# A third fold of seven half-size products, and the MLPs' last sums added at another place

## The chip, the cores and the metric

The kernel runs on one core of a Trainium2 chip. The metric is the device time of one execution in microseconds (us), as the median of several. The engines are named as in the profile: PE is TensorE (matrix products), DVE is VectorE, ACT is ScalarE, POOL is GpSimd, and SP is the engine that issues most DMAs. A bank is one of the eight banks of PSUM, into which PE writes; each holds 128 x 512 float32 numbers.

## The reference

A sequence of 512 tokens with 1024 channels goes through three layers. Their matrices, in the order of the program:

```python
h = layer_norm(a*x + dsa_mixer(x))                 # layer 1, indexed sparse attention
h = layer_norm(a*h + square(relu(h @ w_up)) @ w_down)      # MLP "m1", 4096 hidden
h = layer_norm(a*h + gla_mixer(h))                 # layer 2, gated linear attention
h = layer_norm(a*h + square(relu(h @ w_up)) @ w_down)      # MLP "m2", 4096 hidden
x = x + g1 * (concat(attention(.), mlstm(.)) @ w_out)      # second block
x = x + g2 * ((silu(h @ w_gate) * (h @ w_up)) @ w_down)    # FFN "m3", 2816 hidden
out = rms_norm(x)
```

Everything is float32. The vectors g1, g2 and the shifts and scales of the second block come from one product with w_ada, which the kernel spreads over the MLPs ("ada").

## The kernel before

**Precision.** A float32 product is made of three on PE: each matrix is split into a high half (rounded, written by ACT) and a low half (what is left, written by DVE), and high x high, high x low and low x high are added in a bank. So a weight chunk of 1 MB goes through a fixed row of steps: SP fetches it into one of three `raw` buffers (L3378), ACT writes its high half `wh` (L1482), DVE its low half `wl` (L2212), and PE may read it. A raw buffer is free when its last reader is done, and only then does SP issue the next fetch, in the order of the chunks.

**The MLPs m1 and m2.** The 32 hidden tiles of 128 are worked on in eight units of four. In a cycle PE makes the hidden tiles of unit n (`gemm_T`, L746 to L748) and then the down product of unit n-1. ACT squares the hidden tiles (L1620, L1623). The result is gathered in `h` by DVE (L2428). Some units also carry a chunk of w_ada, which DVE multiplies into `A` (L2198).

**The fold.** For units 1 to 6 the down product, a product of 2x2 blocks, is made by `fold` (L968 to L970) with seven block products P1 to P7 in place of eight (Winograd's scheme): 7 x 12 = 84 matmuls in place of 96. It needs sums of blocks. Those of the hidden tiles are made by POOL (`hidden_sums`), those of the weights by DVE in place in the raw buffers (`weight_sums`, L2413, L2416, L2418, L2421). So a fold has four weight chunks: the left one, the right one with its first sum, the left with its sums, and the last sum; the last two are made of the raw buffers of the first two. P1, P6 and P7 are gathered in one bank after the other ("chain"): P7 may start when DVE has added P6, P6 when it has added P1. P4 and P5 are "lasting": their four banks gather all six units, and DVE adds each of them to two corners of the result at the end of unit 7, six adds L2428 after the last weights.

**The ends of m1 and m2.** Unit 7's down product is made corner by corner: (0,0), (0,1), then (1,0) and so on, a corner being a row block of 128 tokens and half of the channels (`cross` in m1, L770 to L772). While PE is at the next corners, DVE adds the corner to `h` (L2388), takes its statistics (L2270) and, after both halves of a row block, works out the scale of the norm (L2274 to L2288, "scale"). Ahead of the corners stands the ada sum (L906).

**The FFN m3.** Its 22 hidden tiles come in six units, FG = 2, 4, 4, 4, 4, 4 tiles. ACT makes silu(gate), DVE the product with the other branch (L3205) and the low half (L3208). The down product is plain: 22 tiles x 4 x 2 x 3 = 528 matmuls; DVE gathers it (L3188), and in the second-last unit multiplies by g2 and adds to the residual (L3193, L3195). The last unit goes by corners and each is finished at once (L3175, L3178). Two weight slots take turns.

The order of every engine's queue is written out by hand; a helper `take` prepares a fixed number of chunks ahead, and `weights(i)` all up to i.

## Time and profile before

| | |
|---|---|
| median of 3 runs | 1837.14 us (1834.05 to 1839.25) |
| profiled execution | 1838.28 us |
| its span in the trace | 1836.1 us |
| granted TensorE clock, mean | 0.995 |
| PE busy | 1797.3 us, 98% of the span |
| DVE busy | 1248.5 us, 68% |
| ACT busy | 840.4 us, 46% |
| POOL busy | 228.5 us, 12% |

The span lies within the execution, 2.2 us of which are outside it. ACT squares its first hidden tile of m1 at 261 us of the span and of m2 at 871; the last fold of m1 ends at 557 us, that of m2 at 1155; DVE makes the first product of m3 at 1491.

### The profile page before, as it was taken

How to read it: one execution, taken by the hardware profiler on the slowest of the kernel's cores; microseconds unless marked ns; L12 is line 12 of the kernel's file. 1: busy time of each engine (PE TensorE's matmuls, PEld its weight loads, DVE VectorE, ACT ScalarE, POOL GpSimd, SP SyncE). 2: the span in 40 equal slices, each digit the busy share in tenths (PEclk: the TensorE clock that was granted, in tenths of full speed). 3: DMA queues.
4: the chain of work that ended last, by engine and by line, in shares of the span. 5: the costliest groups of instructions: out<-in, count | busy, mean ns of one | idle time of the engine just before them, and what ended most of it. 6: DMA issues, size and time to landing. Idle time of an engine off the chain costs nothing.

```text
span 1836.1 us, 22790 instructions
## 1 busy us (share of the span) xinstructions
PE 1797.3 (98%) x8996; PEld 1465.0 (80%) x8996; DVE 1248.5 (68%) x2048; ACT 840.4 (46%) x1313; POOL 228.5 (12%) x172
## 2 busy tenths in 40 slices
PE   9999999999999999999999999899999999999998
PEld 7775788878887888878888888778757898888886
DVE  4997666888888677476777777886667644433438
ACT  4548453445443443555344444465566442222223
POOL 0241002111110054000222221000012000000001
PEclk9999999999999999999999999999999999999999
DMA  6221405544443121140533433133102313233221
GB/s 215 70 70 36 150 24 184 181 163 138 168 153 117 47 74 65 46 161 24 207 115 115 136 122 133 49 105 102 47 24 70 126 47 115 94 107 98 92 92 46
DMA packets 120330, 189.34 MB, mean 103 GB/s; under 512 B 7816, under 2 KB 72552, under 8 KB 117152
## 3 DMA queue, kind: packets, MB, share of 16 engines
q1 hardware_dynamic: 118688, 182.81, 30.0%
q0 software_dynamic: 1392, 4.82, 0.8%
q8 instruction: 71, 1.16, 0.3%
q14 instruction: 35, 0.29, 0.1%
q10 hardware_dynamic: 144, 0.26, 0.0%
HBM read 185.72 MB, written 2.16 MB: 102 GB/s over the span
## 4 chain that ended last, share of the span: by engine, by line
PE 71%; DVE 16%; DMA 6%; ACT 5%; issue 3%; DVEq 0%; SPq 0%; ACTq 0%
PE bank L746 8%; PE bank L748 8%; PE bank L747 8%; DMA raw<-in_mlp_w_up 4%; DVE wl L2212 3%; PE bank L720 3%; PE bank L722 3%; PE bank L721 3%; PE bank L970 2%; ACT wh L1482 2%; PE bank L968 2%; PE bank L969 2%; DMA raw<-in_mlp_w_down 2%; PE bank L1058 2%; DVE A L2198 2%
## 5 line engine op out<-in xcount | busy, mean ns | idle before, releaser
L2212 DVE TENSOR_TENSOR wl<-raw,wh 128x2048 fp32r<-128x2048 f32 (+2 forms) x161 | 355.2, 2209 | 214.4 <-ACT wh L1482 214.2
L1482 ACT ACTIVATE wh<-raw 128x2048 fp32r<-128x2048 f32 (+1 forms) x166 | 302.0, 1826 | 323.0 <-DMA raw<-in_mlp_w_up 107.4
L746 PE MATMUL bank<-xh,wh 128*128 128x512 f32 (+1 forms) x872 | 341.2, 391 | 0.0
L748 PE MATMUL bank<-xl,wh 128*128 128x512 f32 (+1 forms) x872 | 340.3, 390 | 0.0
L747 PE MATMUL bank<-xh,wl 128*128 128x512 f32 (+1 forms) x872 | 340.3, 390 | 0.0
L746 PEld LDWEIGHTS bank<-xh,wh 128*128 128x128 f32 (+1 forms) x872 | 164.0, 188 | 37.2 <-DVE h L2428 1.7
L748 PEld LDWEIGHTS bank<-xl,wh 128*128 128x128 f32 (+1 forms) x872 | 163.9, 188 | 34.9
L747 PEld LDWEIGHTS bank<-xh,wl 128*128 128x128 f32 (+1 forms) x872 | 164.0, 188 | 34.3
L720 PE MATMUL bank<-wh,xh 128*128 128x512 f32 (+1 forms) x352 | 138.0, 392 | 0.5 <-DVE wl L2212 0.5
L722 PE MATMUL bank<-wh,xl 128*128 128x512 f32 (+1 forms) x352 | 134.1, 381 | 0.0
L721 PE MATMUL bank<-wl,xh 128*128 128x512 f32 (+1 forms) x352 | 133.9, 380 | 0.0
L968 PE MATMUL bank<-wh,uh 128*128 128x512 f32 x336 | 130.8, 389 | 0.1
L969 PE MATMUL bank<-wl,uh 128*128 128x512 f32 x336 | 130.7, 389 | 0.0
L970 PE MATMUL bank<-wh,ul 128*128 128x512 f32 x336 | 130.7, 389 | 0.0
L2428 DVE TENSOR_TENSOR h<-h,bank 128x512 f32<-128x512 f32 x132 | 86.0, 681 | 43.8 <-PE bank L970 43.7
L1584 ACT ACTIVATE A<-bank 128x512 f32<-128x512 f32 (+4 forms) x106 | 51.4, 490 | 74.9 <-PE bank L722 31.8
L1620 ACT ACTIVATE A<-bank 128x512 f32<-128x512 f32 x64 | 38.0, 593 | 90.3 <-PE bank L748 73.8
L720 PEld LDWEIGHTS bank<-wh,xh 128*128 128x128 f32 x352 | 66.2, 188 | 15.1 <-issue 2.6
L722 PEld LDWEIGHTS bank<-wh,xl 128*128 128x128 f32 x352 | 66.1, 188 | 12.8
L721 PEld LDWEIGHTS bank<-wl,xh 128*128 128x128 f32 x352 | 66.2, 188 | 11.5
L848 PE MATMUL bank<-xh,wh 128*128 128x256 f32 x256 | 73.6, 287 | 1.0 <-DVE xl L2263 0.6
L968 PEld LDWEIGHTS bank<-wh,uh 128*128 128x128 f32 x336 | 63.1, 188 | 13.6 <-issue 0.6
(401 smaller groups left out, 3512.3 us busy)
## 6 DMA issues: line engine op xcount, KB each, us to landing
raw<-in_mlp_w_up SPq DMA_DIRECT2D x32, 1024.0 KB, 5.6
raw<-in_mlp_w_down SPq DMA_DIRECT2D x32, 1024.0 KB, 5.2
raw<-in_w_ada SPq DMA_DIRECT2D x24, 1024.0 KB, 5.0
raw<-in_b_w_in SPq DMA_DIRECT2D x12, 1024.0 KB, 5.2
raw<-in_w_gate SPq DMA_DIRECT2D x11, 1024.0 KB, 5.3
raw<-in_w_up SPq DMA_DIRECT2D x11, 1024.0 KB, 5.3
raw<-in_w_in SPq DMA_DIRECT2D x10, 1024.0 KB, 5.0
raw<-in_w_down SPq DMA_DIRECT2D x10, 1024.0 KB, 5.0
```

The lines of the kernel that those rows point to most:

```text
L720: pe.matmul(o, X, H[:, k, :], start=kk == 0, stop=False)
L721: pe.matmul(o, X, L[:, k, :], start=False, stop=False)
L722: step = pe.matmul(o, Y, H[:, k, :], start=False, stop=kk == 7)
L746: pe.matmul(o, H[:, k, c], xh[:, k, :], start=k == 0, stop=False)
L747: pe.matmul(o, L[:, k, c], xh[:, k, :], start=False, stop=False)
L748: step = pe.matmul(o, H[:, k, c], xl[:, k, :], start=False, stop=k == 7)
L968: pe.matmul(o, X, H[:, k0 + k, :], start=not begun and k == 0, stop=False, skip_group_check=on)
L969: pe.matmul(o, X, L[:, k0 + k, :], start=False, stop=False, skip_group_check=on)
L970: step = pe.matmul(o, Y, H[:, k0 + k, :], start=False, stop=ends and k == 1, skip_group_check=on)
L1482: act.activation(slots[slot_of[i]][0][:, 0:n], raw_of(i)[:, 0:n], ACT.Copy).then_inc(*s_high.up(i))
L2212: dve.tensor_tensor(L[:, 0:n], raw_of(i)[:, 0:n], H[:, 0:n].bitcast(F), ALU.subtract).then_inc(*s_low.up(i))
L2428: dve.tensor_tensor(hv, hv, ps, ALU.add).then_inc(*s_row.up(name, ((key, "down", 6), t, c)))
```

## The change

Four things change.

1. m3 has five units, of 4, 4, 4, 4 and 6 tiles. The down product of the first four is made by `fold`, under the key m3, with weight sums, hidden sums on POOL and lasting banks like those of m1; the last unit's six tiles are made directly, corner by corner, 18 matmuls each. There are three weight slots in turn and a sixth slot for the fold's half-size chunk.
2. A fold's chunks stand in another order in all three: left, left with sums, right with its sum, last sum (before: left, right, left with sums, last sum). In m1 and m2 the products come as P1, P2, P6, P5, P7, P4, P3. The left raw buffer is released by the last weight sum, too.
3. In m1 and m2 the lasting sums of P4 and P5 for the row blocks 2 and 3 leave the unit 7: in m1 they are added after the scale of row block 0, in m2 after the norm of row block 0.
4. The four lasting banks go back to the pool of banks only at the end of the last fold.

```diff
-FG = [(0, 2), (2, 4), (6, 4), (10, 4), (14, 4), (18, 4)]
+FG = [(0, 4), (4, 4), (8, 4), (12, 4), (16, 6)]
...
+    def plan_fold(key, d, m, r0):
+
+        folds[key, d] = len(chunks)
+        for c in range(2):
+            plan(m, r0, 4, c * 512, 512)
+            slot_of[len(chunks)] = turn[0]
+            turn.append(turn.pop(0))
+            chunks.append(([], (4, 2)[c], 512))
...
+        def released(i):
+
+            kd, part = fold_of.get(i, (0, None))
+            if part == 0:
+                return [low_of(i + 1), s_step.at(("fold", kd, 3))]
+            return [low_of(i + 1 if part else i)]
...
-        ORDER = (P1, P2, P6, P4, P7, P5, P3)
+        ORDER = {"m1": (P1, P2, P6, P5, P7, P4, P3), "m2": (P1, P2, P6, P5, P7, P4, P3),
+                 "m3": (P1, P2, P6, P4, P7, P5, P3)}
...
-                weights(first + 1)
-                    w.wait_ge(*low_of(first + 1))
-                    dve.tensor_tensor(R0, R1, L0, ALU.subtract).then_inc(*s_step.up(("fold", (key, d), 3)))
-                    weights(first + 2)
...
+            def last_weight_sum(key, d):
+
+                first = folds[key, d]
+                L0, L1, R0, R1 = halves(first)
+                weights(first + 2)
+                w.wait_ge(*low_of(first + 2))
+                dve.tensor_tensor(R0, R1, L0, ALU.subtract).then_inc(*s_step.up(("fold", (key, d), 3)))
...
-                        lasting(P4, 2, 0, True)
-                        lasting(P5, 2, 1, True)
                     owed()
+
+                def last_sums():
+                    lasting(P4, 2, 0, True)
+                    lasting(P5, 2, 1, True)
+
+                return last_sums
...
                     scale(t)
+                    if amid and t == 0:
+                        amid()
                     ada_sum()
...
+            product(0, 0)
+            product(0, 1)
+            cur.take(low)
+            product(0, 2)
+            product(0, 3)
+            cur.take(low)
...
+            cur.take(low, 0)
+            product(LASTF, 4)
+            product(LASTF, 5)
+            gated(3, 0)
+            cur.take(low, 0)
+            last_low(4)
+            last_low(5)
+            gated(3, 1)
+            cur.take(low, 0)
```

`product` is what L3205 does before, `gated` is L3193 and L3195 of before, `last_low` is L3208.

What this does to the queues, at three places. First DVE in a fold of m1, unit 2. wl2 and wl without a number are weight slots; raw<-raw rows are the weight sums. Before, the second L2212 is the right chunk and the third the left with its sums:

```order
L2212 TENSOR_TENSOR wl<-raw,wh 128x2048
L2413 TENSOR_TENSOR raw<-raw 128x1024
L2416 TENSOR_TENSOR raw<-raw 128x1024
L2418 TENSOR_TENSOR raw<-raw 128x1024
L2212 TENSOR_TENSOR wl<-raw,wh 128x2048
L2421 TENSOR_TENSOR raw<-raw 128x1024
L2212 TENSOR_TENSOR wl2<-raw,wh2 128x2048
L2428 TENSOR_TENSOR h<-h,bank6 128x512
```

The same place in the changed kernel (low halves now L2235, sums L2422 to L2435, adds L2448):

```order
L2235 TENSOR_TENSOR wl<-raw,wh 128x2048
L2422 TENSOR_TENSOR raw<-raw 128x1024
L2425 TENSOR_TENSOR raw<-raw 128x1024
L2427 TENSOR_TENSOR raw<-raw 128x1024
L2235 TENSOR_TENSOR wl2<-raw,wh2 128x2048
L2235 TENSOR_TENSOR wl<-raw,wh 128x2048
L2435 TENSOR_TENSOR raw<-raw 128x1024
L2448 TENSOR_TENSOR h<-h,bank6 128x512
```

The low half of the left sums (wl2) has moved from the third place to the first after the three sums; the right chunk and the last sum stand behind it.

Second, DVE at the end of m1, before. The six adds h<-h,bank are P3's (banks 6 and 1) and the four lasting ones (7, 2, 0, 4); wl3 is the last weight chunk of unit 7, the next three are those of the layer after it, L2388 is the first corner:

```order
L2212 TENSOR_TENSOR wl3<-raw,wh3 128x2048
L2428 TENSOR_TENSOR h<-h,bank6 128x512
L2428 TENSOR_TENSOR h<-h,bank1 128x512
L2428 TENSOR_TENSOR h<-h,bank7 128x512
L2428 TENSOR_TENSOR h<-h,bank2 128x512
L2428 TENSOR_TENSOR h<-h,bank0 128x512
L2428 TENSOR_TENSOR h<-h,bank4 128x512
L2212 TENSOR_TENSOR wl<-raw,wh 128x2048 x2
L2212 TENSOR_TENSOR wal<-raw,wal 128x128
L2388 TENSOR_TENSOR h<-h,bank2 128x512
```

In the changed kernel, from the same chunk on:

```order
L2235 TENSOR_TENSOR wl3<-raw,wh3 128x2048
L2442 TENSOR_TENSOR ul<-A,uh 128x512
L2475 TENSOR_TENSOR h<-h 128x512 x2
L2448 TENSOR_TENSOR h<-h,bank6 128x512
L2448 TENSOR_TENSOR h<-h,bank1 128x512
L2235 TENSOR_TENSOR wl<-raw,wh 128x2048 x2
L2235 TENSOR_TENSOR wal<-raw,wal 128x128
L2398 TENSOR_TENSOR h<-h,bank3 128x512
```

and, fifteen small instructions later, at the end of row block 0's scale:

```order
L2338 SCALAR_TENSOR_TENSOR rsa<-rsy,rsh 128x1
L2345 SCALAR_TENSOR_TENSOR small<-rsa,rsy 128x1
L2296 SCALAR_TENSOR_TENSOR small<-mv,small 128x1
L2448 TENSOR_TENSOR h<-h,bank0 128x512
L2448 TENSOR_TENSOR h<-h,bank4 128x512
L2448 TENSOR_TENSOR h<-h,bank7 128x512
L2448 TENSOR_TENSOR h<-h,bank2 128x512
```

Banks 0, 4, 7 and 2 are the lasting ones; their adds stand behind two weight chunks, two corners and a scale. PE's corner (1,0) takes bank 0.

Third, DVE at the start of m3, before (L3205 is a product of hidden tiles, L3208 its low half):

```order
L2212 TENSOR_TENSOR wl<-raw,wh 128x2048
L3205 TENSOR_TENSOR A<-A,bank5 128x512
L3208 TENSOR_TENSOR ul<-A,uh 128x512
L3205 TENSOR_TENSOR A<-A,bank7 128x512
L3208 TENSOR_TENSOR ul<-A,uh 128x512
L2212 TENSOR_TENSOR wl<-raw,wh 128x2048
L2212 TENSOR_TENSOR wl<-raw,wh 128x2048
L3205 TENSOR_TENSOR A<-A,bank0 128x512
```

and in the changed kernel, where the third L2235 is the gate chunk of unit 1:

```order
L2235 TENSOR_TENSOR wl2<-raw,wh2 128x2048
L3198 TENSOR_TENSOR A<-A,bank7 128x512
L3198 TENSOR_TENSOR A<-A,bank6 128x512
L2235 TENSOR_TENSOR wl<-raw,wh 128x2048
L3198 TENSOR_TENSOR A<-A,bank2 128x512
L3198 TENSOR_TENSOR A<-A,bank5 128x512
L2235 TENSOR_TENSOR wl<-raw,wh 128x2048
```

A chunk that PE reads next stands ahead of the products of hidden tiles before, and behind them now. In the last unit of the changed kernel the same holds for a down chunk (L3198 are the products of tiles 4 and 5, L3235 and L3237 a `gated`):

```order
L2235 TENSOR_TENSOR wl<-raw,wh 128x2048
L3198 TENSOR_TENSOR A<-A,bank2 128x512
L3198 TENSOR_TENSOR A<-A,bank5 128x512
L3235 TENSOR_TENSOR A<-A 128x512
L3237 TENSOR_TENSOR h<-h,A 128x512
L2235 TENSOR_TENSOR wl2<-raw,wh2 128x2048
L3242 TENSOR_TENSOR ul<-A,uh 128x512 x2
```

The first L2235 is the chunk of tiles 0 and 1, the second that of tiles 2 to 5 for the left half of the channels.

## Rows read from the trace of the kernel before

**Rows 1.** The page's line of PE and the others: busy time and share of the span by engine.

```profile
PE 1797.3 (98%) x8996; PEld 1465.0 (80%) x8996; DVE 1248.5 (68%) x2048; ACT 840.4 (46%) x1313; POOL 228.5 (12%) x172
```

**Rows 2.** Waits of PE, longest first: us in total, times, longest.

```profile
PE bank L906 <- DVE h L2428: 3.7, 1, 3.7
PE bank L770 <- DVE h L2428: 3.5, 1, 3.5
```

**Rows 3.** Timeline of PE: start us, us, instruction; a fold's start and end, another's P6.

```profile
331.86 0.39 PE L968 MATMUL bank<-wh,uh 128*128 128x512 f32 x1
...
350.89 0.39 PE L746 MATMUL bank<-xh,wh 128*128 128x512 f32 x1
...
378.33 0.47 PE L968 MATMUL bank<-wh,uh 128*128 128x512 f32 x1
```

**Rows 4.** Timeline of DVE in m1's folds, last one m2's; in brackets idle time before, and releaser.

```profile
377.51 1.28 DVE L2428 TENSOR_TENSOR h<-h,bank 128x512 f32<-128x512 f32 x2
...
449.03 1.23 DVE L2413 TENSOR_TENSOR raw<-raw 128x1024 f32<-128x1024 f32 x1 [0.37 <-DMA raw<-in_mlp_w_down]
...
451.62 1.23 DVE L2418 TENSOR_TENSOR raw<-raw 128x1024 f32<-128x1024 f32 x1
452.77 2.28 DVE L2212 TENSOR_TENSOR wl<-raw,wh 128x2048 fp32r<-128x2048 f32 x1
455.09 1.23 DVE L2421 TENSOR_TENSOR raw<-raw 128x1024 f32<-128x1024 f32 x1
456.23 2.28 DVE L2212 TENSOR_TENSOR wl<-raw,wh 128x2048 fp32r<-128x2048 f32 x1
...
466.23 2.73 DVE L2212 TENSOR_TENSOR wl<-raw,wh 128x2048 fp32r<-128x2048 f32 x1 [0.82 <-ACT wh L1482]
468.87 3.38 DVE L2198 SCALAR_TENSOR_TENSOR A<-raw,small,A 128x2048 f32<-128x2048 f32 x1
...
489.94 1.23 DVE L2413 TENSOR_TENSOR raw<-raw 128x1024 f32<-128x1024 f32 x1 [0.51 <-DMA raw<-in_mlp_w_down]
...
1013.83 0.69 DVE L2428 TENSOR_TENSOR h<-h,bank 128x512 f32<-128x512 f32 x1 [3.39 <-PE bank L970]
```

**Rows 5.** Timeline of SP and of ACT in the same fold: fetches and high halves.

```profile
458.54 0.37 SPq L3378 DMA_DIRECT2D raw<-in_mlp_w_up  x1
...
452.88 1.92 ACT L1482 ACTIVATE wh<-raw 128x2048 fp32r<-128x2048 f32 x1 [0.67 <-DVE raw L2418]
...
464.20 1.92 ACT L1482 ACTIVATE wh<-raw 128x2048 fp32r<-128x2048 f32 x1 [1.59 <-DMA raw<-in_mlp_w_up]
```

**Rows 6.** Timelines of ACT, DVE and PE at the end of m1.

```profile
560.28 1.91 ACT L1482 ACTIVATE wh<-raw 128x2048 fp32r<-128x2048 f32 x1 [1.01 <-DMA raw<-in_b_w_in]
...
568.96 0.69 DVE L2388 TENSOR_TENSOR h<-h,bank 128x512 f32<-128x512 f32 x1 [0.47 <-PE bank L772]
...
572.45 0.16 DVE L2288 SCALAR_TENSOR_TENSOR small<-mv,small 128x1 f32<-128x1 f32 x1
...
569.12 0.47 PE L770 MATMUL bank<-wh,uh 128*128 128x512 f32 x1
```

**Rows 7.** End of m2: DVE and PE timelines; windows (us, busy and count by engine, PEclk).

```profile
1157.20 3.67 DVE L2428 TENSOR_TENSOR h<-h,bank 128x512 f32<-128x512 f32 x6
...
1159.13 0.80 PE L770 MATMUL bank<-wh,uh 128*128 128x512 f32 x1 [3.54 <-DVE h L2428]
...
1164.42 0.46 PE L770 MATMUL bank<-wh,uh 128*128 128x512 f32 x1
...
1169.00:1202.00 33.00, 30.84 (x144) 24.27 (x144) 30.23 (x73) 16.68 (x35) 0.00 (x0) 1.00 0.10 32
...
1159.00:1163.00 4.00, 3.87 (x9) 3.11 (x10) 4.00 (x6) 1.88 (x3) 0.00 (x0) 0.50 0.48 133
```

**Rows 8.** m3: a window of it, and one instruction of DVE's timeline.

```profile
1490.00:1829.00 339.00, 338.84 (x1501) 280.47 (x1500) 149.35 (x164) 91.21 (x95) 9.05 (x7) 1.00 0.28 90
...
1507.92 0.69 DVE L3205 TENSOR_TENSOR A<-A,bank 128x512 f32<-128x512 f32 x1 [0.64 <-PE bank L748]
```

More of the change, by code:

```diff
@@ new lines, in silu @@
+            def silu(n, i):
+                q, j = i // 2, i % 2
+                w.wait_ge(*s_gemm.at((("gate", n, q), j)))
+                if i > 3:
+                    w.wait_ge(*s_xlow.at(("m3", "u", i - 4)))
+                elif n:
+                    w.wait_ge(*s_xlow.at(("m3", "U", n - 1, P3 if q else P5)))
+                act.activation(rb[:, i % 4, :], bank[banks.of[("gate", n, q), j]][:, :], ACT.Silu).then_inc(*s_act.up(("gate", n, i)))
+                banks.read[("gate", n, q), j] = s_act.at(("gate", n, i))
@@ new lines, in scalar_program @@
+            cur.take(high)
+            high_of("m3", 0, P1)
+            high_of("m3", 0, P4)
+            high_of("m3", 0, P2)
+            for n in range(1, LASTF):
+                first = folds["m3", n - 1]
+                cur.take(high, 0)
+                cur.take(high, 0)
+                for s in (P6, P7, P5, P3):
+                    high_of("m3", n - 1, s)
+                cur.take(high, 0)
+                silu(n, 0)
+                silu(n, 1)
+                cur.take(high, 0)
+                weights(first)
+                silu(n, 2)
+                silu(n, 3)
+                weights(first + 2)
+                high_of("m3", n, P4)
+                high_of("m3", n, P1)
+                weights(first + 3)
+                high_of("m3", n, P2)
+                cur.used = first + 4
+                weights(first + 5)
@@ new lines, in scalar_program @@
+            first = folds["m3", LASTF - 1]
+            cur.take(high, 0)
+            cur.take(high, 0)
+            for s in (P6, P7, P5, P3):
+                high_of("m3", LASTF - 1, s)
+            weights(first)
+            silu(LASTF, 0)
+            silu(LASTF, 1)
+            weights(first + 3)
+            cur.used = first + 4
+            cur.take(high, 0)
+            cur.take(high, 0)
+            last_high(0)
+            last_high(1)
+            cur.take(high, 0)
+            silu(LASTF, 2)
@@ new lines, in vector_program, with added @@
+            last = {}
+            def added(d, s):
+                t0, c = TO[s]
+                for t in (t0, t0 + 1):
+                    name, where = ("m3", "Q", d, s, t - t0), sum_of("m3", d, s, t - t0)
+                    ps = bank[banks.of[where]][:, :]
+                    w.wait_ge(*s_gemm.at(("m3", "P", d, s, t - t0)))
+                    if (t, c) in last:
+                        w.wait_ge(*s_row.at(last[t, c]))
+                        dve.tensor_tensor(fv(t, c), fv(t, c), ps, ALU.add).then_inc(*s_row.up(name))
+                    else:
+                        dve.tensor_copy(fv(t, c), ps).then_inc(*s_row.up(name))
+                    last[t, c] = name
+                    if s in (P2, P7, P3):
+                        banks.read[where] = s_row.at(name)
@@ new lines, in lasting @@
+            def lasting(s, t0, c, base):
+                for t in (t0, t0 + 1):
+                    name, where = ("m3", "E", s, t, c), sum_of("m3", LASTF - 1, s, t - t0)
+                    w.wait_ge(*s_gemm.at(("m3", "P", LASTF - 1, s, t - t0)))
+                    w.wait_ge(*s_row.at(last[t, base]))
+                    dve.tensor_tensor(fv(t, c), fv(t, base), bank[banks.of[where]][:, :], ALU.add).then_inc(*s_row.up(name))
+                    last[t, c] = name
+                    if t0:
+                        banks.read[where] = s_row.at(name)
@@ new lines, in vector_program @@
+            d, first = LASTF - 1, folds["m3", LASTF - 1]
+            cur.take(low, 0)
+            cur.take(low, 0)
+            for s in (P6, P7, P5, P3):
+                low_half_of("m3", d, s)
+            weight_sums("m3", d)
+            weights(first + 1)
+            product(LASTF, 0)
+            product(LASTF, 1)
+            added(d, P1)
+            last_weight_sum("m3", d)
+            added(d, P2)
+            added(d, P6)
+            weights(first + 3)
+            added(d, P7)
@@ new lines, in vector_program @@
+            weights(first + 4)
+            lasting(P5, 0, 1, 1)
+            lasting(P5, 2, 1, 0)
+            lasting(P4, 2, 0, 0)
+            cur.used = first + 4
+            cur.take(low, 0)
+            cur.take(low, 0)
+            last_low(0)
+            last_low(1)
+            added(d, P3)
+            gated(0, 0)
+            gated(1, 0)
+            cur.take(low, 0)
+            gated(0, 1)
+            product(LASTF, 2)
+            product(LASTF, 3)
+            gated(1, 1)
+            cur.take(low, 0)
@@ L3357, in gpsimd_program @@
             pool.dma_start(fg, final_norm_g_2.partition_broadcast(P)).then_inc(s_gb, 16)
+            for d in range(LASTF):
+                hidden_sums("m3", d)
             w.wait_ge(s_gb, 16 * G_FIN)
@@ L3411, in sync_program @@
             for before, i in zip(fetched, fetched[NRAW:]):
-                w.wait_ge(*low_of(before + 2 if before in fold_of else before))
+                for read in released(before):
+                    w.wait_ge(*read)
                 fetch(i)
```

466 lines of the change are left out of this document (217 added, 249 removed).

## The prediction

> **What bounds the kernel now.** I read the page's busy shares first: PE is busy 98% of the span [rows 1]. PE is the bound, and a change pays if it takes matmuls away or fills PE's gaps; DVE and ACT matter where they make PE wait. The matmul's price comes from starts, since their shown durations overlap: a fold of 84 starts at 331.86 and what follows it at 350.89, so 19.03/84 = 0.2266 us each [rows 3]. Next, PE's waits, longest first. The two longest are 3.7 and 3.5 us, for adds of DVE at the ends of m1 and m2 [rows 2]; six such adds stand there in one row of 3.67 us [rows 7].
>
> Then I looked for what nearly bounds PE, since such a thing turns into a wait when it is moved. It is in m1's folds. Follow one weight buffer through the timelines [rows 4, 5]: the first sum L2413 starts at 449.03, three sums run to 452.85, the right chunk's low half, the last sum and the left sums' low half follow with no gap to 458.51; SP fetches the next chunk into the buffer just freed at 458.54; it has landed and ACT starts on it at 464.20, idle before that for the DMA; DVE's low half starts at 466.23, idle before that for ACT; an L2198 of 3.38 us ends at 472.25 and frees the next buffer; two more fetches later the next first sum starts at 489.94, again idle before that for its DMA. No step of this ring waits for PE, and its round takes 40.91 us. PE's own cycle there is 96 matmuls of hidden tiles and 84 of the fold, 180 x 0.2266 = 40.8 us. The two are equal: the ring has no slack. In one fold it already shows: DVE's two adds of P1 start at 377.51, and PE's P6, which waits for the first, starts at 378.33, 0.24 us later than the pitch puts it [rows 3, 4].
>
> **The change, part by part.** All differences are against the profiled execution, 1838.28 us (span 1836.1); the median of the runs is 1837.14, 1.1 lower.
>
> *Fewer matmuls in m3.* Sixteen tiles in four folds: 4 x 84 = 336; six tiles direct: 6 x 24 = 144; 480 in place of 528. 48 x 0.2266 = -10.9 us, all on the path: in m3 PE is busy 338.84 of 339 us [rows 8]. The sums, hidden sums and adds that pay for it lie on DVE, ACT and POOL; DVE is busy there only 149 of 339 us, so I cost them at nothing, but for the two places below. The corners at the end are longer than DVE's work on them; I take -0.4 for the 0.5 us by which DVE is late there.
>
> *The start of m3.* The low half of unit 1's gate chunk is now queued behind the products of tiles 2 and 3 (third place of the order above). The last product waits for PE's last matmul before that chunk, and PE needs the chunk at once: signal 0.1 + product 0.69 [rows 8] + low half 2.28 [rows 4] = +3.1 us.
>
> *The last unit.* Tile 5's product can start when the matmuls of hidden tiles end. PE then has tiles 0 and 1 of the first corner, 6 matmuls, 1.36 us. The next chunk's low half comes after the product, a `gated` pair and nothing shorter: 0.1 + 0.69 + 2 x 0.69 (a `gated` pair has the same shape) + 2.28 = 4.45, less 1.36 = +3.1 us [rows 4, 8].
>
> *The clock after these two.* After m2's gap of 3.54 us the granted clock was 0.50, the 1.2 GHz level: twelve matmuls from 1159.13 to 1164.42, 5.29 in place of 2.72, so 2.57 lost [rows 7]. A gap of 3.1 us isn't in the trace of m3; nearest above is this one (2.57 each), nearest below 0. I take 1 each, +2. The Trainium skill (TensorE: Matmul & The Clock Gate, Part 1) says that the half rate is the default and activity releases it, so that idleness brings it back. By that both gaps cost the full price and the sum would be 3 us higher; the trace agrees for m2's gap and leaves the shorter one open.
>
> *m1's folds.* Here the change harms, I think. The left sums' low half stands now directly after the three sums, ahead of the right chunk (first place of the order). ACT can start its high half only at 452.88, when the last of the three sums is written, and takes 1.92 [rows 5]: DVE sits idle from 452.85 to about 454.9. Before, the right chunk's low half filled that time. All behind it, the right chunk, the last sum, and the release of the left buffer that now waits for that last sum, comes 2.1 us later (458.5 to 460.6). In a ring with no slack that is 2.1 us a round, and there are six folds: 12.6 us at the end of m1. PE takes the delay as waits ahead of P6 and P7, whose banks wait for DVE's adds. Bounds: 0, if the ring slides into slack that I do not see (shorter DMAs, POOL no longer beside L2212 and L2198, which take 2.73 and 3.38 there [rows 4]), and 12.6. No row shows slack, so I take 12.6.
>
> *The end of m1.* The wait of 3.7 us goes, but the corner (1,0) now takes a lasting bank, and its add stands behind two weight chunks, two corners and the scale of row block 0. The second chunk's high half ends at 562.19 for want of its DMA [rows 6]; low half 2.28 and 0.29 for the small one, to 564.8; two corners with statistics, 4 x 0.7 with hand-overs, 567.6; the scale's small steps, 2.2 by the rows from the second statistics on (the whole of second corner and scale is 568.96 to 572.61, 3.65 [rows 6]), 569.8; one lasting add, 0.7, and a signal: 570.9 to 571.1. Before, (1,0) started at 569.12 [rows 6]: +1.9. PE has by then been idle since the corner (0,1), some 7 us, and starts at half rate: +2.6, as at m2 [rows 7]. Together +4.5, and with the folds +17.1.
>
> *The end of m2.* In its units DVE waits 3.39 us for PE ahead of P1's adds [rows 4], so there the new order is hidden. The gap of 3.54 and the slow matmuls behind it, 2.57, go: up to -6.1, less some 1 us for P3's adds, -5.1. But the four lasting adds, 4 x 0.65 = 2.6 us (3.67 for six [rows 7]), move into the chain of norms, and DVE is busy 30.2 of the 33 us after that [rows 7]: the chain bounds that stage. Net between -5.1 and -2.5; I take -3.0.
>
> Sum: -10.9 - 0.4 + 3.1 + 3.1 + 2 + 17.1 - 3.0 = +11.0. 1838.3 + 11.0 = 1849.3 for a profiled execution, 1848.2 for the median. Own range: m1's ring at half of its price (-6.3), gaps at 0 or at full clock price (-2 to +3), m2 at either end (-2.1 to +0.5): about 1838 to 1854.
>
> **The rivals.**
>
> *The ring has slack (0.18).* The chunks' order in m1 costs nothing. For: DMA times vary, and POOL's share of the slow L2198 can move away. Against: the idle time of DVE ahead of each step of the ring is put down to DMA and ACT, never to PE. Then the sum is 11.0 - 12.6 = -1.6, a median of 1835.5: not slower. It decides from a slack of some 2 us in each round.
>
> *As meant (0.12).* Neither ring nor new waits: the adds come late enough to harm nobody, and low halves are ready in m3. -10.9 - 0.4, m2 -5.1, m1's gap of 3.7 and its cold matmuls, some -1.5 (L906's eight in 1.94 us and so on): -5.2. Together -21.6: 1815.5. For: PE in m3 has no wait now and DVE is idle more than half of the time. Against: the three places in the orders; each of the queues is served in order.
>
> *m3's waits hidden, ring as I say (0.08).* If the chunks' low halves were ready early, the 8.2 us of the two gaps and their clock go: +2.8, 1840.
>
> *The ring costs more than its round (0.05).* A late ring also makes PE cold in the folds: its waits of up to 3.9 us would each add up to 2.57. Two such: 1853; four: 1858.
>
> **How the numbers follow.** Forecast 0.57, and the rivals above. A change of 0.3% (5.5 us: 1831.6 to 1842.7) is about what a measurement of this kernel can tell. Faster: the intended case, 0.12, and a quarter of the slack case, 0.04: 0.16. Same: the rest of the slack case, 0.14, most of the 1840 case, 0.06, and the forecast's low end, 0.04: 0.24. Slower: 0.60. The range 1832 to 1856 leaves out the intended case, the lowest of the slack case and the highest of the last, about 0.2.
>
> **What would show it.** Each step has its mark in the profile after. Sums: the DVE starts of the first weight sum in m1 stand 42.9 us apart and not 40.8; DVE idles about 2 us, for ACT, ahead of the low half after the three sums; PE waits in m1's folds for L2448 of P1 or P6, some 10 us in all; PE's corner (1,0) of m1 waits for L2448 some 7 us, and the granted clock is 0.5 behind it; no such wait at m2. In m3 PE waits twice for L2235, about 3 us each, and nowhere else; the last fold of m3 to the end is otherwise shorter by 48 pitches. If the first sums still stand 40.8 apart, the ring is wrong and the time is near 1835; if PE has no wait for L2235 in m3, the reading of the orders is.

## The result and the profile after

| | before | changed |
|---|---|---|
| median of 6 runs | 1837.56 us | 1847.08 us |
| ratio | | 1.0055 (95%: 1.0042 to 1.0068) |
| span of the profiled execution | 1836.1 us | 1845.4 us |
| PE busy | 1797.3 us | 1791.4 us |

The kernel is slower, by 9.5 us between the two medians, although PE has 48 matmuls less to do. (Before was timed three more times beside the changed kernel, so its median differs from the 1837.14 above.) The page's line of busy times after, which answers to [rows 1]:

```profile
PE 1791.4 (97%) x8948; PEld 1455.0 (79%) x8948; DVE 1291.6 (70%) x2089; ACT 854.8 (46%) x1332; POOL 260.3 (14%) x188
```

PE's waits after, us in total, times, longest. Against [rows 2], the adds at the two ends (L2428 before, L2448 now) are still there, others are new:

```profile
PE bank L778 <- DVE h L2448: 7.2, 2, 6.5
PE bank L948 <- DVE h L2448: 4.4, 5, 1.1
PE bank L754 <- DVE wl L2235: 3.5, 2, 3.0
...
PE bank L1442 <- DVE wl L2235: 3.0, 1, 3.0
...
PE bank L948 <- ACT A L1612: 1.7, 2, 1.5
```

L778 are the corners at the end of m1 and m2, L948 the folds, L754 a hidden product of m3 and L1442 its last unit.

**m1's ring.** DVE's timeline in a fold of m1, to be laid beside [rows 4]. The third weight sum ends at 459.1; DVE then waits 1.98 us for ACT's high half of the left sums, and only then come both low halves (x2) and the last sum. The lines after it are the first weight sums of this fold and the next two, then ACT's two high halves (x2), back to back, and the fetch that the last sum releases:

```profile
457.88 1.23 DVE L2427 TENSOR_TENSOR raw<-raw 128x1024 f32<-128x1024 f32 x1
461.09 4.49 DVE L2235 TENSOR_TENSOR wl<-raw,wh 128x2048 fp32r<-128x2048 f32 x2 [1.98 <-ACT wh L1477]
465.62 1.23 DVE L2435 TENSOR_TENSOR raw<-raw 128x1024 f32<-128x1024 f32 x1
...
455.30 1.23 DVE L2422 TENSOR_TENSOR raw<-raw 128x1024 f32<-128x1024 f32 x1 [0.69 <-DMA raw<-in_mlp_w_down]
498.47 1.23 DVE L2422 TENSOR_TENSOR raw<-raw 128x1024 f32<-128x1024 f32 x1 [0.41 <-DMA raw<-in_mlp_w_down]
541.55 1.23 DVE L2422 TENSOR_TENSOR raw<-raw 128x1024 f32<-128x1024 f32 x1 [0.40 <-DMA raw<-in_mlp_w_down]
...
459.14 3.73 ACT L1477 ACTIVATE wh<-raw 128x2048 fp32r<-128x2048 f32 x2 [4.83 <-DVE raw L2427]
...
466.92 0.37 SPq L3496 DMA_DIRECT2D raw<-in_mlp_w_up  x1
```

A round takes 43.2 and 43.1 us in place of 40.9 [rows 4]; over the five rounds of m1 it is 43.3 on the mean, against 41.1 before. What the left sums' wait adds on DVE comes back on PE as waits at P6 and P7. PE's timeline, m1, with two of the folds' waits, and one of another kind, for ACT's hidden tile (L1612), which now stands behind those two high halves:

```profile
378.59 0.47 PE L948 MATMUL bank<-wh,uh 128*128 128x512 f32 x1 [1.51 <-ACT A L1612]
...
510.76 0.47 PE L948 MATMUL bank<-wh,uh 128*128 128x512 f32 x1 [1.10 <-DVE h L2448]
...
553.84 0.47 PE L948 MATMUL bank<-wh,uh 128*128 128x512 f32 x1 [1.10 <-DVE h L2448]
```

**m1's end.** PE, DVE and a window (its PEclk is the third number from the right) after:

```profile
583.36 0.79 PE L778 MATMUL bank<-wh,uh 128*128 128x512 f32 x1 [6.53 <-DVE h L2448]
...
582.55 0.16 DVE L2296 SCALAR_TENSOR_TENSOR small<-mv,small 128x1 f32<-128x1 f32 x1
582.63 2.48 DVE L2448 TENSOR_TENSOR h<-h,bank 128x512 f32<-128x512 f32 x4
...
580.00:584.00 4.00, 0.64 (x2) 0.54 (x3) 3.65 (x15) 1.24 (x1) 0.00 (x0) 0.50 1.09 366
```

The corner (1,0) starts at 583.36, behind the first of the four moved adds, which stand behind the scale: 14.24 us later than its twin at 569.12 [rows 6].

**m3.** PE and DVE at its start and in its last unit. The low half stands right behind a product at the start of m3 and behind a product and a `gated` pair in the last unit, and PE starts as it ends:

```profile
1527.46 0.50 PE L754 MATMUL bank<-xh,wh 128*128 128x512 f32 x1 [2.98 <-DVE wl L2235]
...
1805.71 0.79 PE L1442 MATMUL bank<-wh,uh 128*128 128x512 f32 x1 [2.95 <-DVE wl L2235]
...
1524.51 0.69 DVE L3198 TENSOR_TENSOR A<-A,bank 128x512 f32<-128x512 f32 x1 [4.75 <-PE bank L756]
1525.12 2.29 DVE L2235 TENSOR_TENSOR wl<-raw,wh 128x2048 fp32r<-128x2048 f32 x1
...
1803.37 2.28 DVE L2235 TENSOR_TENSOR wl<-raw,wh 128x2048 fp32r<-128x2048 f32 x1
```

**A table by stage.** I took three marks of PE that both kernels have: the first 128x256 matmul after m1, the first 128x272 matmul some 55 us after m2's corners begin, and the last x8 transposes but one ahead of m3.

| mark | before, us | changed, us | later by |
|---|---|---|---|
| after m1 | 587.72 | 603.52 | 15.8 |
| after m2's end | 1215.00 | 1227.10 | 12.1 |
| ahead of m3 | 1469.45 | 1480.60 | 11.2 |
| end of the span | 1836.1 | 1845.4 | 9.3 |

So m1 lost 15.8 us, m2's end gave back 3.7, a stage whose own code the change does not touch 0.9, and m3 gave 1.9 of its 10.9.

### The profile page after: what moved, and what is told of

Its sections match the earlier page's. It is cut to its first block, busy times and chain, and to the rows that moved or that the text cites. A ratio compares the mean times of both kernels' runs of the same rounds, so it can differ in the third digit from the quotient of the medians.

```text
span 1845.4 us, 22761 instructions
## 1 busy us (share of the span) xinstructions
PE 1791.4 (97%) x8948; PEld 1455.0 (79%) x8948; DVE 1291.6 (70%) x2089; ACT 854.8 (46%) x1332; POOL 260.3 (14%) x188
## 4 chain that ended last, share of the span: by engine, by line
PE 70%; DVE 16%; ACT 6%; DMA 5%; issue 3%; DVEq 0%; SPq 0%; ACTq 0%
PE bank L754 9%; PE bank L756 9%; PE bank L755 9%; PE bank L948 4%; PE bank L950 4%; PE bank L949 4%; DVE wl L2235 3%; DMA raw<-in_mlp_w_up 3%; PE bank L728 3%; PE bank L730 3%; PE bank L729 3%; ACT wh L1477 3%; PE bank L1039 2%; PE bank L1023 2%; PE bank L1014 2%
## 5 line engine op out<-in xcount | busy, mean ns | idle before, releaser
L2235 DVE TENSOR_TENSOR wl<-raw,wh 128x2048 fp32r<-128x2048 f32 (+2 forms) x164 | 366.1, 2240 | 162.5 <-ACT wh L1477 162.3
L1477 ACT ACTIVATE wh<-raw 128x2048 fp32r<-128x2048 f32 x169 | 308.8, 1838 | 353.5 <-DMA raw<-in_mlp_w_up 111.1
L754 PE MATMUL bank<-xh,wh 128*128 128x512 f32 (+1 forms) x872 | 342.2, 392 | 3.5 <-DVE wl L2235 3.5
L754 PEld LDWEIGHTS bank<-xh,wh 128*128 128x128 f32 (+1 forms) x872 | 164.4, 189 | 41.4 <-DVE wl L2235 4.3
L948 PE MATMUL bank<-wh,uh 128*128 128x512 f32 x432 | 169.5, 392 | 6.6 <-DVE h L2448 4.4
L949 PE MATMUL bank<-wl,uh 128*128 128x512 f32 x432 | 168.3, 389 | 0.0
L950 PE MATMUL bank<-wh,ul 128*128 128x512 f32 x432 | 168.2, 389 | 0.0
L2448 DVE TENSOR_TENSOR h<-h,bank 128x512 f32<-128x512 f32 x132 | 85.0, 680 | 33.2 <-PE bank L950 33.0
L3376 POOL TENSOR_TENSOR A<-A 128x512 f32<-128x512 f32 x16 | 23.0, 1438 | 592.5 <-DVE ul L2410 592.5
L948 PEld LDWEIGHTS bank<-wh,uh 128*128 128x128 f32 x432 | 81.1, 188 | 28.6 <-issue 9.3
L950 PEld LDWEIGHTS bank<-wh,ul 128*128 128x128 f32 x432 | 81.1, 188 | 17.1
L949 PEld LDWEIGHTS bank<-wl,uh 128*128 128x128 f32 x432 | 81.1, 188 | 16.4
L1602 ACT ACTIVATE uh<-A 128x512 fp32r<-128x512 f32 x112 | 63.3, 619 | 38.3 <-POOL A L3382 18.2
L2410 DVE TENSOR_TENSOR ul<-A,uh 128x512 fp32r<-128x512 f32 x112 | 74.9, 712 | 6.3 <-ACT uh L1602 6.2
```

Of the source, the lines that this page charges most:

```text
L754: pe.matmul(o, H[:, k, c], xh[:, k, :], start=k == 0, stop=False)
L948: pe.matmul(o, X, H[:, k0 + k, :], start=not begun and k == 0, stop=False, skip_group_check=on)
L949: pe.matmul(o, X, L[:, k0 + k, :], start=False, stop=False, skip_group_check=on)
L950: step = pe.matmul(o, Y, H[:, k0 + k, :], start=False, stop=ends and k == 1, skip_group_check=on)
L1477: act.activation(slots[slot_of[i]][0][:, 0:n], raw_of(i)[:, 0:n], ACT.Copy).then_inc(*s_high.up(i))
L2235: dve.tensor_tensor(L[:, 0:n], raw_of(i)[:, 0:n], H[:, 0:n].bitcast(F), ALU.subtract).then_inc(*s_low.up(i))
```

## The experiments

The time of before, measured beside each of them, was 1837.5 to 1838.4 us. The edits are against the changed kernel, unless said, and are shown in part.

### The chunks' order of m1 and m2 undone

```diff
+RIGHT_FIRST = ('m1', 'm2')
...
+        if key in RIGHT_FIRST:
+            s = turn[:]
+            turn[:] = [s[0], s[2], s[1], s[3]]
+            for c in range(2):
+                plan(m, r0, 4, c * 512, 512)
+            for nk in (4, 2):
+                slot_of[len(chunks)] = turn.pop(0)
+                chunks.append(([], nk, 512))
+            return
         for c in range(2):
             plan(m, r0, 4, c * 512, 512)
```

The places that name a fold's second or third chunk follow.

> The changed kernel with one thing undone in m1 and m2: a fold's chunks stand again as left, right, left with sums, last sum, so that DVE and ACT work on the right chunk while the left sums are finished. The products' order, the moved lasting sums and all of m3 stay as changed. My theory (the ring of m1 has no slack and pays some 2.1 us in each of six folds): first weight sums 40.8 us apart again, no idle time of DVE after the three sums, no wait of PE for adds inside m1's folds, corner (1,0) of m1 at about 571 us and not 583.4; the time falls by about 12 us, to 1835. The rival (the products' new order or the lasting banks held to the end cause m1's waits): no change, 1847. A second rival (the ring is late for its DMAs and only drifts): half, 1841.

Measured: 1832.94 us, ratio to before 0.9976 (0.9965 to 0.9987), 14.1 us less than the changed kernel. The first weight sums are back where they were: 489.88 here, 489.94 before [rows 4]. Its DVE and PE timelines:

```profile
489.88 1.23 DVE L2444 TENSOR_TENSOR raw<-raw 128x1024 f32<-128x1024 f32 x1 [0.48 <-DMA raw<-in_mlp_w_down]
...
569.91 0.79 PE L798 MATMUL bank<-wh,uh 128*128 128x512 f32 x1 [5.80 <-DVE h L2472]
...
591.30 0.36 PE L871 MATMUL bank<-xh,wh 128*128 128x256 f32 x1 [0.20 <-DVE xl L2292]
```

The mark after m1 is at 591.30 and not 603.52: the order alone costs 12.2 us there. It builds up in two steps and is then made a little smaller by chance. The last fold ends 10.7 us later in the changed kernel (the matmul after it starts at 567.65, here at 556.93). Corner (1,0) starts 13.5 us later (583.36 against 569.91), since in the changed kernel PE also waits 1.95 us ahead of corner (0,0) for a low half of a hidden tile, L2442, that DVE reaches late. Behind the corner PE's slow matmuls lost 1.6 us in the changed kernel and 2.9 in this one (569.91 to 575.96 for fourteen), which takes 1.3 off again.

The products' order and the late release of banks, which are still in, cost no wait in the folds but one of 0.75 us. No run has the new products' order alone. What is left of m1's loss, 591.30 against 587.72, is 3.6 us, with PE's wait of 5.8 us for the moved sums.

Of the 14.1 us by which the time fell, 12.2 are this. Another 1.4 lie in m3, whose code is that of the changed kernel; the section on m3's low halves says where they come from.

### A delay of known size in the ring, and the same outside it

Against the kernel before, in m1 or in m2:

```diff
                     w.wait_ge(*s_step.at(("T2", key, d)))
+                    if key == "m1":
+                        dve.tensor_tensor(L1, L1, L1, ALU.max).then_inc(*s_step.up(("again", key, d)))
+                        w.wait_ge(*s_step.at(("again", key, d)))
```

> The kernel before, with one more instruction of DVE in each of m1's six folds, ahead of the third weight sum: it writes the right-hand half of the left raw buffer onto itself (maximum of it with itself, 128x1024, about 1.3 us with its wait). Nothing else changes. It prices the ring. My theory (no slack at all): the first weight sums stand 42.1 us apart in place of 40.8, and the time grows by 6 x 1.3 = 7.9 us, to 1845.5. The rival (some slack of 1 us or more in each round): at most 2 us, 1839.

> The kernel before with the same extra instruction of DVE (half of the left raw buffer onto itself, 128x1024) in each of m2's six folds and none in m1's. A control for the delay in m1, which cost 6.3 us. My theory (m2's folds have slack, since DVE waits 3.4 us for PE in them): no change, 1837.5 (+-1.5). The rival (any delay of DVE in a fold costs its own length, whatever the ring): +6 us, 1843.5.

Measured: in m1 1843.78 us, 1.0034 (1.0021 to 1.0047), +6.3 us; in m2 1838.29 us, 1.0003 (0.9994 to 1.0012), +0.7, which can't be told from none. Six instructions of the same size cost 1.0 us each in one MLP and, by the interval, at most 0.4 in the other. With six more instructions m1's first weight sums start at 324.80 and 535.25, five rounds, 42.1 us each on the mean; at before the same five took 325.46 to 530.77, 41.1 each. In m2 the first weight sums stay as far apart as before: 920.55 to 1129.51 over five rounds, 918.89 to 1128.01 without the added instruction. The added instruction takes 1.25 us from its start to the next one's. DVE's timeline in m1, where L2419 is the added one:

```profile
454.32 1.23 DVE L2419 TENSOR_TENSOR raw<-raw 128x1024 f32<-128x1024 f32 x1
455.57 1.23 DVE L2421 TENSOR_TENSOR raw<-raw 128x1024 f32<-128x1024 f32 x1
```

So a round grows by 1.0 us for 1.25 added: the ring has about 0.2 us of slack, not the 1 or more of the rival. PE feels it in full only behind the folds: the last one ends 3.4 us later than before (560.42 against 556.98), PE then waits 5.8 us for DVE's adds where before waits 3.7, and the mark after m1, 594.73, is 7.0 us later.

### The two low halves of m3 moved ahead

```diff
             cur.take(low)
+            cur.take(low)
             product(0, 2)
             product(0, 3)
-            cur.take(low)
...
             cur.take(low, 0)
+            cur.take(low, 0)
             product(LASTF, 4)
             product(LASTF, 5)
             gated(3, 0)
-            cur.take(low, 0)
```

> The changed kernel with two low halves of weights moved on DVE and nothing else: at the start of m3 the gate chunk of unit 1 ahead of the products of tiles 2 and 3, in the last unit the down chunk of tiles 2 to 5 ahead of the products of tiles 4 and 5. My theory: both waits of PE for a low half (3.0 and 3.0 us) vanish and the clock stays at 1.00 behind them (1.75 and 1.45 us of slow matmuls), 9.4 us less, 1837.7. The rival (what stands behind the low half is late next: products, ACT's high halves or a bank): a new wait of 1 to 3 us takes the place of each, 1840 to 1845.

Measured: 1838.87 us, 1.0007 (0.9997 to 1.0017), 8.2 less than the changed kernel. A window of m3 in it shows PE without a wait and the clock at its full level:

```profile
1480.00:1830.00 350.00, 349.60 (x1641) 293.26 (x1640) 204.42 (x230) 122.88 (x139) 37.66 (x23) 1.00 0.27 88
```

From the last mark ahead of m3 (1483.58 here) to the end of its span, 1839.2, it takes 355.6 us, where the changed kernel takes 364.8 and before 366.7: 9.2 less than the one and 11.0 less than the other. That is the whole of the 48 matmuls, with nothing late behind the two low halves. The median shows 1 us less of it. Its profiled execution came out of m1 3.9 us later than that of the changed kernel (607.42) and stood 3.0 later ahead of m3; the executions of any one kernel here lie 1.7 to 6.3 us apart.

The clock's share of the 9.2 us is not the same each time. The kernel with the chunks' order undone and the one with m1's sums back (next section) have the same two gaps in m3, but in each of them the clock fell behind one gap only, and the other cost nothing beyond its own length. So their m3 takes 363.4 and 363.5 us, 1.3 to 1.4 less than the 364.8 above. The gap in the last unit of the first of them, and a window from the same start (PEclk, the third number from the right, is 1.00):

```profile
1792.75 0.50 PE L1463 MATMUL bank<-wh,uh 128*128 128x512 f32 x1 [2.95 <-DVE wl L2256]
1793.09 0.39 PE L1464 MATMUL bank<-wl,uh 128*128 128x512 f32 x1
1793.32 0.39 PE L1465 MATMUL bank<-wh,ul 128*128 128x512 f32 x1
...
1792.75:1796.75 4.00, 4.00 (x18) 3.30 (x19) 3.96 (x5) 0.39 (x2) 0.00 (x0) 1.00 0.00 0
```

### m1's lasting sums back in unit 7

```diff
                         added(d, P3)
+                        if key in ('m1',):
+                            lasting(P4, 2, 0, True)
+                            lasting(P5, 2, 1, True)
                     owed()
...
                 def last_sums():
-                    lasting(P4, 2, 0, True)
-                    lasting(P5, 2, 1, True)
+                    if key not in ('m1',):
+                        lasting(P4, 2, 0, True)
+                        lasting(P5, 2, 1, True)
```

> The changed kernel with the four lasting sums of row blocks 2 and 3 back in unit 7 of m1, ahead of the next weights; m2 and m3 as changed. My theory: PE's wait of 6.5 us ahead of corner (1,0) and the 1.5 us of slow matmuls behind it go, since the adds end at about 575 us, before corner (0,1) does (576); the weights and norms behind them on DVE are 2.5 us later, which hides behind PE; 7 us less, 1840. The rival (the late ring, not the place of the sums, sets the end of m1, through the next weights and the norm of row block 0): at most 2 us less, 1845.

Measured: 1843.72 us, 1.0029 (1.0016 to 1.0042), 3.4 less than the changed kernel, between the two. The wait at the corner (1,0) is gone, as I said, but more than half of it (3.9 of 6.5 us) comes back as a wait for the norm of row block 0, whose scale the four adds have pushed back (ACT's L1546 writes the normed rows, L796 transposes them):

```profile
586.44 1.94 PE L796 MATMUL bank<-C,h 128*128 128x128 f32 x8 [3.91 <-ACT h L1546]
```

The mark after m1 is 2.4 us earlier (601.14). Two things bound m1's end at nearly the same time, the bank and the scale. Before the change PE had one wait there, of 3.7 us ahead of the ada sum, and none over 1 us behind it.

### The moved sums alone

Against the kernel before:

```diff
-                        lasting(P4, 2, 0, True)
-                        lasting(P5, 2, 1, True)
                     owed()
+
+                def last_sums():
+                    lasting(P4, 2, 0, True)
+                    lasting(P5, 2, 1, True)
...
-                    if d == 6 and s in LASTING:
+                if d == 6:
+                    for s in LASTING:
                         for r in range(2):
                             banks.drop(sum_of(key, d, s, r))
```

with the two calls of `last_sums` as in the change.

> The kernel before with one part of the change alone: the lasting sums of row blocks 2 and 3 are added behind the scale of row block 0 in m1 and behind its norm in m2, and the four lasting banks are given back at the end of the last fold. Chunks, products and m3 as before. My theory of the prediction: m1 +4.5, m2 -3.0, together +1.5, 1839. With what the changed kernel without its ring delay showed (m1's exit 3.6 us later than before, m2's end 3.5 us earlier): 0, 1837.5. The rival (the moved sums are a clear gain, PE's two waits of 3.7 and 3.5 us go): -6, 1831.5.

Measured: 1836.99 us, 0.9998 (0.9988 to 1.0008): no difference that can be told. The mark after m1 is at 590.15, 2.4 later than before, the one after m2 at 1214.35, so the stretch between them gave back 3.1. PE's longest wait, and the start of m2's corner (0,0), which now follows the last fold with no wait:

```profile
570.05 0.80 PE L770 MATMUL bank<-wh,uh 128*128 128x512 f32 x1 [5.95 <-DVE h L2431]
...
1157.62 0.39 PE L770 MATMUL bank<-wh,uh 128*128 128x512 f32 x1
```

Corner (1,0) of m1 starts at 570.05, 0.9 us later than before, and eight slow matmuls behind it (to 573.47) lose 1.6; these two are the 2.4. In the kernel with the chunks' order undone the same corner starts at 569.91, 0.8 later than before, and the slow matmuls lose 2.9: these are its 3.6.

### All three harms out, and m3 alone

The first kernel joins the three edits above (m2's sums stay moved). The second is the same with m2's sums back as well, so that only m3, the products' order and the banks' late release differ from before.

> The changed kernel with all three harms taken out: chunks' order of m1 and m2 as before, both low halves of m3 ahead of the products, and m1's lasting sums back in unit 7 (m2's stay moved). If the parts add up: 1832.9 (the first alone) - 8.2 (the second alone) - 3.6 (m1's exit at its time of before) = 1821. The rival (the parts overlap: PE's time that one sets free is lost to another's wait): 1825 or more.

> m3 of the changed kernel alone, with both low halves ahead of the products; in m1 and m2 the chunks' order and the place of the lasting sums are those of before. If the parts add: 48 matmuls and the tail, 1837.6 - 10.9 - 0.4 = 1826.3, and 3 to 6 above the kernel with m2's moved sums (1820.5). The rival (m2's moved sums give nothing by themselves, and the gain came from m1's products or banks): 1820 to 1822.

Measured: 1820.54 us, 0.9913 (0.9898 to 0.9927), and 1822.49 us, 0.9917 (0.9902 to 0.9932). The first is at the 1821 that was expected if the parts add up. Some 2 us of that are luck with the clock: from the mark after m1 to the end of m2's last fold it takes 565.5 us and before 567.7, and the granted clock from 600 to 660 us is 1.00 in the first and 0.94 in the other. The same kernel once more took 1824.55 (below), so "adds up" holds to some 4 us. The second is only 2 above the first, where moving m2's sums should have made 3 to 6. With such a spread the totals can't decide that; its PE timeline can:

```profile
1155.07 0.39 PE L798 MATMUL bank<-wh,uh 128*128 128x512 f32 x1
...
1209.61 0.39 PE L748 MATMUL bank<-wh,xh 128*128 128x272 f32 x1 [0.48 <-DVE wl L2256]
```

Corner (0,0) of m2 starts right behind the last fold, at 1155.07, with no wait, though the four sums are made ahead of the next weights, as before. In [rows 7] it waits 3.54 us for them. What differs is which bank it takes. The pool hands out banks in the order in which they came back; with the lasting banks given back at the end of the fold only, the corners (0,0) and (0,1) take the two of P1, P6 and P7, and the first lasting bank goes to row block 2.

The products' order of m2 is changed here too, but it is not what took the wait away: the kernel with the moved sums alone has the old order, the late release and no wait either (1157.62). By the program, the new order with the early release would still give corner (0,0) a lasting bank, one of P5's; no run shows that one.

From the start of corner (0,0) to the mark after m2 are 54.5 us, where before has 59.6 from the end of its last fold (1155.43 to 1215.00), and the kernel with m2's sums moved 56.0:

```profile
1153.06 0.39 PE L798 MATMUL bank<-wh,uh 128*128 128x512 f32 x1
...
1209.10 0.39 PE L748 MATMUL bank<-wh,xh 128*128 128x272 f32 x1 [0.51 <-DVE wl L2256]
```

These stretches hardly vary. All eight profiles with the new products' order and m2's sums moved give 56.0, the changed kernel's among them, and the two with m2's sums in unit 7 give 54.5. Of the 59.6 of before, 2.6 are the slow matmuls behind the gap; the two kernels with a delay, whose end of m2 is that of before, have the same gap of 3.54, lose 1.7 and 1.8 behind it, and need 58.6. So the banks' release is worth 4.1 to 5.0 us, and moving the sums costs 1.5 of it.

### P4's sums early, P5's late; and both ends

Of m1's four sums only P5's two stay behind the scale. In the last kernel m2's four stand in unit 7 too. Its edit, where `last_sums` keeps what is left:

```diff
                         added(d, P3)
+                        lasting(P4, 2, 0, True)
+                        if key == "m2":
+                            lasting(P5, 2, 1, True)
                     owed()
```

> As the kernel with all three harms taken out, but of m1's four lasting sums only the two of P4, whose banks corners (1,0) and (1,1) take, stand in unit 7; the two of P5 stay behind the scale of row block 0. My theory (at the end of m1 two things bound: the bank of (1,0), and the chain to the scale of row block 0, which waits for the next weights' DMA): PE starts the corners some 2 us earlier than before and loses at most 1 to the scale, 1819 to 1820. The rival (the chain to the scale alone bounds, so that when the sums are added makes no difference): 1821, as the one with all four.

> The kernel with all three harms taken out, once more beside the next one, in more rounds: 1820.5.

> The same with only P4's two sums in unit 7 of m1, once more. Its profiled execution was 1.9 us shorter at m1's exit (585.6 against 587.5 us); if that is the sums' place, its median is 1 to 2 us below the other's; if it is chance, they are equal.

> The changed kernel with the chunks' order of before in m1 and m2 and both low halves of m3 ahead; of the lasting sums only m1's two of P5 stay moved, all four of m2 are back in unit 7. The run of m3 alone showed corner (0,0) of m2 starting with no wait though no sum was moved, and the stretch from there to the next stage 54.5 us, against 56.0 with the sums moved and 59.6 before. My theory now: m2's gap went because the lasting banks are given back last, so that the first corners take others, and moving the sums into the chain of norms costs 1.5 us. So this one is 1.5 us below its twin with m2's sums moved (1820.1 and 1821.4): 1819, with that stretch at 54.5. The rival (the stretch was shorter by chance, or by another stage): 1820 to 1821, and 56.0.

Measured: P4's early 1820.13 us, 0.9906 (0.9892 to 0.9921); again 1821.35, 0.9908 (0.9895 to 0.9922); all harms out once more 1824.55, 0.9922 (0.9909 to 0.9934); both ends 1820.54, 0.9900 (0.9884 to 0.9917). The intervals overlap, so the totals don't tell these four apart. The 1819 that was expected of the last is not shown either; in its profiled execution the stretch between the mark after m1 and m2's last fold took 567.5 us at a granted clock of 0.94 (600 to 660 us), 2.0 more than in the other three, at 1.00. The stretches tell more: with both ends as described, corner (0,0) of m2 at 1154.55 and the mark at 1209.10, 54.55 us, as expected:

```profile
1154.55 0.39 PE L798 MATMUL bank<-wh,uh 128*128 128x512 f32 x1
...
1209.10 0.39 PE L748 MATMUL bank<-wh,xh 128*128 128x272 f32 x1 [0.49 <-DVE wl L2256]
```

The mark after m1 was at 585.6 and 585.1 with P4's sums early, at 587.0 in the last kernel, which has the same m1, and at 587.5, 589.5 and 589.7 without. PE's wait for the norm of row block 0 was 2.3, 2.4 and 2.6 us in the three with P4's sums early and 3.7, 3.9 and 3.9 in the three without, so that wait is 1.4 us shorter. In two of the first three the clock did not fall there either, in all of the others it did. That the total time falls by it is likely and not shown. These versions are 0.8 to 1.0% faster than before and 1.2 to 1.5% faster than the change.

## Why the prediction was right

It gave 1848 us and slower; measured were 1847.08. The three places in the queues, and what each does to PE, were read rightly, and they carry the result. That the number came within 1.1 us is partly luck, since several terms were off by 1 us or more and cancelled. Point by point, in the order of its sum:

- **48 matmuls, -10.9, tail -0.4.** Right: with both waits out, m3 is 11.0 us shorter than before.
- **Start of m3 and last unit, +3.1 each.** Right to the step: 1524.09, the last matmul's start, to 1527.46 is 3.37, less the pitch of 0.23 is 3.1; 1802.37 to 1805.71 is 3.34, again 3.1. Moving the two low halves took both away, with nothing late behind.
- **The clock behind them, +2.** Too small in the changed kernel: 1.75 and 1.45 us, read from where the matmuls' starts are 0.2266 apart again (1532.61, fifteen matmuls; 1809.43, ten). In the two other kernels with the same gaps it was 1.7 and 1.8 in all, since only one gap brought the low level. So 0 or some 1.6 for each gap, and the 1 each that was taken lies between. The Trainium skill (TensorE: Matmul & The Clock Gate, Part 1) has the half rate as the default that activity releases. The prediction read it as: both gaps bring it back, at the full price of 2.57 each. Four of the six gaps seen did, at 1.45 to 1.75 us.
- **m1's ring, +12.6.** Right in mechanism and nearly in size: 12.2 at the mark after m1, by undoing the order alone. But only 10.7 of it is there at the end of the last fold, where I had all of it; the rest comes at corner (0,0), as a wait for a late low half that I had not seen. The idle time of DVE was 1.98 where I had 2.0 to 2.1, the round 43.1 to 43.2 where I had 42.9. "No slack" was nearly right; the dosed delay showed 0.2 us. I had not seen either that a hidden tile comes late behind ACT's two high halves, now back to back (1.5 us once); a part of that is the ring's lateness, since the delay alone, with the halves apart, makes the same tile 1.1 us late.
- **m1's end, +4.5.** Somewhat too large: 3.6 with the changed order of products (591.30), 2.4 alone (590.15). The corner (1,0) came at 583.36, where 569.12 + 12.6 + 1.9 gives 583.6, but that is two errors that cancel. With the ring as before the corner is 0.8 to 0.9 later and not 1.9, and the ring makes it 13.5 later and not 12.6. The working's own numbers (569.8, an add of 0.7 and a signal of 0.1) give 570.6 and not 570.9 to 571.1, and 569.91 and 570.05 were measured. The clock behind the wait was 1.6 us in the changed kernel (583.36 to 587.03 for nine matmuls) and with the sums alone, and 2.9 with the order undone, where 2.6 was taken: the difference between 3.6 and 2.4 is this clock.
- **m2's end, -3.0.** The size was nearly right (3.5 less from the end of the last fold, 3.7 with the stretch before it), the reason was wrong, and that is luck. I let the gap go because the sums are moved. It goes because the banks are given back later; moving the sums costs 1.5 of the 4.1 to 5.0 us that the banks give.
- **The rivals.** Slack in the ring: refuted by the kernel with the order undone and by the delay. As meant: no. m3's waits hidden: no. The ring costs more than its round: no, the granted clock stayed at 1.00 through m1's folds (325 to 567 us).
- **The range.** Its terms, -10.4 and +3.5 around 1848.2, give 1838 to 1852; the 1854 at the upper end is not what they add up to. The result lies in both.

Sum of what was measured by stage: +15.8 - 3.7 - 0.9 - 1.9 = +9.3, against +11.0. The 0.9 us between the marks 1215.00 and 1469.45 is in a stage whose code is the same in both kernels. It goes with the late release of the banks: that stage takes 254.4 to 254.6 us in before and the two kernels with a delay, and 253.3 to 253.9 in all others, the moved sums alone (253.9) among them. Why it does is not shown.

The waits list alone would have misled: it shows 6.1 us of waits in the folds (4.4 and 1.7), while the last fold ended 10.7 us later (the matmul after it at 567.65; before, 556.98 by the pitch). A wait is counted there from the modelled end of the matmul before, 0.39 us after its start, so each is some 0.16 us too small and short ones vanish; the distances of starts in m1's folds sum up to 11.6 us over the pitch, against 1.1 before.

## What to carry to other kernels

Before a step is reordered, follow one buffer once around, from fetch to release, and note what ended the idle time ahead of each of its steps. If none of them is the bounding engine and the round is as long as that engine's cycle, what is put into the ring is paid nearly in full once per round (here 1.0 of 1.25 us), while the same instruction in a loop with a wait for the bounding engine cost nothing that could be told. When an engine's queue is written by hand, put what the bounding engine reads next ahead of what depends on its last result. When a wait goes away, check by undoing each part which of them took it away: here the release of banks did, and the step that was meant to do it cost time. And compare stretches of the trace with the granted clock beside them: a fall of the clock that comes or stays away by chance is worth 1 to 3 us here, as much as several of the parts.

## What the runs showed of the hardware

- A gap of PE of some 3 us could make the granted clock fall or not: of six such gaps in m3, in three kernels with the same m3, four did. The fall could come after the work had resumed: after the gap that ended at 1527.46 the first five matmuls started 0.23 to 0.34 apart, the next eight 0.39 to 0.43, and then 0.23 again. PE's timeline of the changed kernel:

```profile
1528.28 0.40 PE L754 MATMUL bank<-xh,wh 128*128 128x512 f32 x1
1528.51 0.48 PE L755 MATMUL bank<-xh,wl 128*128 128x512 f32 x1
1528.78 0.63 PE L756 MATMUL bank<-xl,wh 128*128 128x512 f32 x1
1529.21 0.63 PE L754 MATMUL bank<-xh,wh 128*128 128x512 f32 x1
...
1531.77 0.55 PE L754 MATMUL bank<-xh,wh 128*128 128x512 f32 x1
1532.16 0.39 PE L755 MATMUL bank<-xh,wl 128*128 128x512 f32 x1
```

- The time lost at the low level behind a gap did not follow from the gap's length: 1.75 and 1.45 us behind 3.1, 1.6 behind 6.5, 2.9 behind 5.8 and, behind the same wait of 3.54 at the end of m2, 2.6 before [rows 7] but 1.7 and 1.8 in the two kernels with a delay.
- One more DVE instruction of 1024 columns per fold cost 1.0 us a piece in m1; in m2 all six cost 0.7 us, with an interval from -1.1 to 2.2, which can't be told from nothing.
- Which of the eight banks a product took decided whether PE waited: with the four lasting banks last in the pool, m2's first corner started with no wait, where it had waited 3.54 us.
